# Two convolution projection chunks of a Conformer/MoBA block as one seven-product block

## The chip, the cores and the metric

The kernel is one launch on one core of one Trainium2 chip. The metric is the device time of that launch in microseconds, the median of several runs. Everything is float32 in and out. A matrix product is made of three TensorE products of float32r parts (high x high, low x high, high x low).

## The reference

A decoder block on x (256 tokens of 2048 columns): a SwiGLU feed-forward network, a token mixer, a second feed-forward network, each with a residual and a layer norm. The mixer's input projection has 12288 columns; its `u` part feeds the convolution.

```python
z = h @ w_in
q, k, v, u, ga, gc = jnp.split(z, list(np.cumsum(IN_SPLITS)[:-1]), axis=-1)
o = moba_attention(to_heads(q), to_heads(k), to_heads(v))
y_attn = o.transpose(0, 2, 1, 3).reshape(B, S, ATTN_WIDTH) @ w_attn_out
# conformer_conv
a, g = jnp.split(u, 2, axis=-1)
h = a * jax.nn.sigmoid(g)
h = conv_general_dilated(h, w_dw, 31 causal taps per channel, 1024 channels) + b_dw
h = jax.nn.silu(layer_norm(h, ln_g, ln_b))
y_conv = h @ w_pw2
return (jax.nn.sigmoid(ga) * y_attn + jax.nn.sigmoid(gc) * y_conv) @ w_out
```

## The kernel before

**Groups.** Weights come in groups of 4 row blocks of 128 by 512 columns (1 MB). For group n, SyncE loads it into one of eight slots `g_raw`, ScalarE writes its high part (`g_split`, L817) and VectorE the low part (`g_lo_of`, L1338) into place n % 4 of a ring (`RING` = 4), and TensorE multiplies it with the token factors `xF_hi`/`xF_lo` (L2259 to L2261). ScalarE may write group n only when TensorE has finished group n-4 (`g_used`), and a slot is loaded again when the low part of its last user is made. All four engines and the queues walk orders written out by hand, and semaphores tie them.

**Direct and seven-product.** A chunk is 512 columns of the projection. Direct, it takes four groups, each against both token tiles: 24 matmuls a group. In a "full" block two chunks (g and u) share a Strassen-Winograd scheme of seven products with 14 groups of 12 matmuls, P1a to P4b, where a and b are the two halves of a product's depth. The scheme needs sums of weight groups. VectorE makes some in place (`add`, L1346, semaphore `t_ready`), GpSimd makes others by a DMA that reads a group from memory and adds it onto a slot (`add_from_hbm`, L2102). It also needs copies of PSUM banks (`fork`, L899) and subtractions (`values`, L1819).

**The mixer's order.** After the first network's norm come the convolution's four chunks, all direct: gate columns, value columns, for the first and the second 512 channels (`CONV_CHUNKS`). ScalarE takes the sigmoid (`conv_gate`, L1084), VectorE the product (`conv_value`, L1760), TensorE turns it (`turn_conv`, L2245) and ScalarE puts it into `ch` (`conv_block`, L1077). Then six blocks of the mixer (`mixing_block`), each the 14 groups of two chunks and 4 direct groups Q1 to Q4 of a third. Blocks 0 to 3 project the keys, values and queries of four heads each; blocks 4 and 5 project gate columns. The attention of the four heads of block g-1 runs inside block g (blocks 1 to 4, the head blocks): keys and queries are transposed by VectorE (L1824), written to memory and read back by GpSimd's queue (L2140, L2147), copied by ScalarE (`qT`, L1108) and multiplied by TensorE (`scores`, L2544). Then eight direct groups of gate columns (the gate groups), then `attn_out`, `conv_out` and `mix_out`, whose weights go in units through `raw`, `w_hi`, `w_lo` (L767, L1315), and whose four `attn_out` chunks share one pair of banks that VectorE empties (`attn_rows`, L1950).

**Taps.** The 31 taps of each of 8 channel tiles are 248 VectorE instructions on 128x256 (L1774, L1777), two tiles in turn with one accumulator each (`cacc`). They are spread by hand over the VectorE order: 33 around the last convolution groups, 16 in block 0, 16 in each head block, 17 in the last block, 8 or 6 behind each gate group, 3 behind each unit of `attn_out`, the last 2 at one place in its third chunk:

```python
lo_conv(13)
dve.wait_ge(cw_loaded, 32)
dve.wait_ge(kept_out, 16 * TT * ND)
taps(11)
lo_conv(14)
taps(11)
lo_conv(15)
taps(11)
```

`BLOCK_TAPS` gives ten places a block: behind Q1, P5a, P3b, P7b, Q3, P4a, P2a, P2b, P4b and behind `values`.

## Time and profile before

| | us |
|---|---|
| median of 3 runs | 2113.19 (2112.93 to 2113.49) |
| span of the profiled execution | 2109.5 |
| TensorE busy | 2095.7 (99%) |
| TensorE weight loads busy | 1734.6 (82%) |
| VectorE busy | 1877.2 (89%) |
| ScalarE busy | 1402.9 (67%) |
| GpSimd busy | 216.7 (10%) |
| DMA engines, mean | 264 GB/s |

The span runs from the first to the last instruction of one profiled execution; the median of the timed runs lies 3.7 us above it, and no other time is known of that execution. Matmuls overlap in the record, so TensorE's pace is read from the distance between their starts. In a timeline the number in brackets is the engine's idle time before a row, with what ended it.

### The profile page before, as it was taken

To read this page: it belongs to the slowest core of one execution; us is meant where nothing else is said; L and a number is where in the kernel's file an instruction comes from. 1 tells how busy PE (TensorE), PEld (TensorE's weight loads), DVE (VectorE), ACT (ScalarE), POOL (GpSimd) and SP (SyncE) were. 2 spreads that over 40 slices of the span, in tenths; PEclk is the share of its full clock that TensorE was granted. 3 is DMA by queue.
4 is the path that set the end of the run, shared out by engine and by line. 5 is a ranking of instruction groups with operands and counts; after the bars stand their busy time and mean duration, and the time that the engine had idled before them with its cause. 6 is when DMAs were issued, how large, how long until landed. Compare 5 with 4: busy or idle time off the path is not lost.

```text
span 2109.5 us, 23778 instructions
## 1 busy us (share of the span) xinstructions
PE 2095.7 (99%) x9386; PEld 1734.6 (82%) x9386; DVE 1877.2 (89%) x1420; ACT 1402.9 (67%) x1313; POOL 216.7 (10%) x345
## 2 busy tenths in 40 slices
PE   9999999999999999999999999999999999999998
PEld 7888888888888888888888888888888888888886
DVE  7899999999996889999999986659899999999996
ACT  6677777777775546766676445335677777777773
POOL 0111111101110001011100000000111111100110
PEclk9999999999999999999999999999999999999999
DMA  9798988888985759998898556755788988899892
GB/s 369 253 295 260 279 270 266 291 300 277 289 279 231 276 158 311 299 269 270 304 301 262 212 185 240 260 178 200 244 294 255 282 272 267 290 302 278 288 285 113
DMA packets 92397, 556.65 MB, mean 264 GB/s; under 512 B 13056, under 2 KB 13440, under 8 KB 35200
## 3 DMA queue, kind: packets, MB, share of 16 engines
q1 hardware_dynamic: 68544, 437.69, 54.7%
q0 software_dynamic: 23744, 117.46, 25.8%
q8 instruction: 74, 1.21, 0.2%
q14 instruction: 35, 0.29, 0.0%
HBM read 534.13 MB, written 20.97 MB: 263 GB/s over the span
## 4 chain that ended last, share of the span: by engine, by line
PE 88%; DVE 8%; DMA 2%; ACT 1%; issue 1%; SPq 0%; DVEq 0%; ACTq 0%
PE acc L2259 14%; PE acc L2261 14%; PE acc L2260 14%; PE tb L2259 12%; PE tb L2261 12%; PE tb L2260 12%; PE acc L2197 3%; PE acc L2199 3%; PE acc L2198 3%; DVE g_lo L1338 3%; DVE cacc L1777 3%; DMA g_raw<-in_groups 1%; PE tb L2245 1%; DVE w_lo L1315 1%; DVE g_raw L1346 1%
## 5 line engine op out<-in xcount | busy, mean ns | idle before, releaser
L1338 DVE TENSOR_TENSOR g_lo<-g_raw,g_hi 128x2048 fp32r<-128x2048 f32 x506 | 1147.6, 2286 | 120.4 <-ACT g_hi L817 119.8
L817 ACT ACTIVATE g_hi<-g_raw 128x2048 fp32r<-128x2048 f32 x506 | 964.4, 1916 | 319.8 <-DVE g_raw L1346 121.5
L2259 PE MATMUL acc<-g_hi,xF_hi 128*128 128x512 f32 x1184 | 464.3, 392 | 0.6 <-ACT acc L899 0.6
L2261 PE MATMUL acc<-g_hi,xF_lo 128*128 128x512 f32 x1184 | 461.1, 389 | 0.0
L2260 PE MATMUL acc<-g_lo,xF_hi 128*128 128x512 f32 x1184 | 460.7, 389 | 0.0
L2259 PE MATMUL tb<-g_hi,xF_hi 128*128 128x512 f32 x760 | 296.3, 390 | 0.3 <-DVE g_lo L1338 0.2
L2261 PE MATMUL tb<-g_hi,xF_lo 128*128 128x512 f32 x760 | 295.7, 389 | 0.0
L2260 PE MATMUL tb<-g_lo,xF_hi 128*128 128x512 f32 x760 | 295.7, 389 | 0.0
L1346 DVE TENSOR_TENSOR g_raw<-g_raw,g_raw 128x2048 f32<-128x2048 f32 x120 | 274.3, 2286 | 1.3
L2259 PEld LDWEIGHTS acc<-g_hi,xF_hi 128*128 128x128 f32 x1184 | 222.3, 188 | 46.8 <-ACT acc L899 1.0
L2261 PEld LDWEIGHTS acc<-g_hi,xF_lo 128*128 128x128 f32 x1184 | 222.2, 188 | 46.8
L2260 PEld LDWEIGHTS acc<-g_lo,xF_hi 128*128 128x128 f32 x1184 | 222.4, 188 | 45.1
L2259 PEld LDWEIGHTS tb<-g_hi,xF_hi 128*128 128x128 f32 x760 | 142.7, 188 | 30.4 <-issue 1.1
L2261 PEld LDWEIGHTS tb<-g_hi,xF_lo 128*128 128x128 f32 x760 | 142.6, 188 | 29.8
L2102 POOL DMA_DIRECT2D g_raw<-in_groups x80 | 72.5, 941 | 918.8 <-DVE g_lo L1338 870.6
L2260 PEld LDWEIGHTS tb<-g_lo,xF_hi 128*128 128x128 f32 x760 | 142.7, 188 | 29.4
L767 ACT ACTIVATE w_hi<-raw 128x1024 fp32r<-128x1024 f32 x80 | 84.7, 1062 | 105.0 <-DMA raw<-in_stream 65.4
L2259 PE MATMUL tb<-g_hi,hT_hi 128*128 128x512 f32 x384 | 149.8, 390 | 0.0
L2261 PE MATMUL tb<-g_hi,hT_lo 128*128 128x512 f32 x384 | 149.4, 389 | 0.0
L2260 PE MATMUL tb<-g_lo,hT_hi 128*128 128x512 f32 x384 | 149.4, 389 | 0.0
L2259 PE MATMUL acc<-g_hi,hT_hi 128*128 128x512 f32 x320 | 124.7, 390 | 0.0
L2261 PE MATMUL acc<-g_hi,hT_lo 128*128 128x512 f32 x320 | 124.5, 389 | 0.0
(180 smaller groups left out, 2307.7 us busy)
## 6 DMA issues: line engine op xcount, KB each, us to landing
g_raw<-in_groups SPq DMA_DIRECT2D x356, 1024.0 KB, 7.2
g_raw<-in_groups POOLq DMA_DIRECT2D x80, 1024.0 KB, 8.6
raw<-in_stream SPq DMA_DIRECT2D x80, 512.0 KB, 4.5
bounce<-h_sq POOLq DMA_DIRECT2D x40, 256.0 KB, 5.5
h_in<-bounce POOLq DMA_DIRECT2D x160, 64.0 KB, 2.6
ln_gb<-in_ln SPq DMA_DIRECT2D x6, 1024.0 KB, 6.6
g_raw<-in_groups SPq DMA_DIRECT2D x6, 512.0 KB, 9.7
res<-in_x_rows SPq DMA_DIRECT2D x1, 2048.0 KB, 16.6
```

Source lines behind the costliest of these rows:

```text
L767: act.activation(w_hi[:, seg.split(j)], raw[:, seg.raw(j)], ACT.Copy).then_inc(hi_ready, 1)
L817: act.activation(g_hi[:, n % RING], source[:], ACT.Copy).then_inc(g_hi_ready, 1)
L1338: dve.tensor_tensor(g_lo[:, n % RING], source[:], f32(g_hi[:, n % RING]), ALU.subtract).then_inc(g_lo_ready, 1)
L1346: dve.tensor_tensor(out[:], a[:], b[:], ALU.add).then_inc(t_ready, 1)
L1777: ins = dve.scalar_tensor_tensor(out=rows if j == TAPS - 1 else cacc[:, k], in0=rows, scalar=w, in1=cacc[:, k], op0=ALU.mult, op1=ALU.add)
L2102: pool.dma_start(out=source(f, b, onto)[:].rearrange("p k n -> p (k n)"), in_=groups[k], accum_op=ALU.add).then_inc(ready, 16)
L2197: pe.matmul(out_ap, x[0][:, k, rows], w_hi[:, s, cols], start=begin, stop=False)
L2198: pe.matmul(out_ap, x[0][:, k, rows], w_lo[:, s, cols], start=False, stop=False)
L2199: return pe.matmul(out_ap, x[1][:, k, rows], w_hi[:, s, cols], start=False, stop=end)
L2259: pe.matmul(bank, x_hi_ap, g_hi[:, n % RING, blk], start=begin, stop=False, skip_group_check=True)
L2260: pe.matmul(bank, x_hi_ap, g_lo[:, n % RING, blk], start=False, stop=False, skip_group_check=True)
L2261: return pe.matmul(bank, x_lo_ap, g_hi[:, n % RING, blk], start=False, stop=end, skip_group_check=True)
```

## The change

The convolution's third and fourth chunk (gate and value columns of the second 512 channels) are no longer two direct chunks of four groups but one seven-product block of 14 groups, `conv_pair`, numbered block -1. Two of its sums are T1a and T1b (`add` of ra onto qa, rb onto qb), two more T2a and T2b, all on VectorE, and four are adding DMAs. Its value part comes out of `values` into `vt`, its gate part out of two sigmoids (`conv_gate_out`) into `k_sb`, and their product is made in block 0 behind Q1 (`conv_pair_value`). TensorE turns it there behind Q1 too, where it stood ahead of Q1. The 33 taps that stood around the last convolution groups go: 3 to block 0, 3 to each of the four head blocks, 3 to the last block, 8 to the gate groups, and 7 are left over for the place of the last ones in `attn_out`, which has 9 now. `TAP_ROUNDS` still takes the tiles two by two with two accumulators. `SPLIT0` and the counts of some semaphores follow the new number of groups.

```diff
-SPLIT0 = 2
+SPLIT0 = 6
...
+PAIR = ("P1a", "P1b", "P5a", "P5b", "P6a", "P3a", "P6b", "P3b", "P7a", "P7b", "P2a", "P4a", "P4b", "P2b")
+PAIR_LOADS = {"qa": "P4a", "ra": "P7a", "qb": "P4b", "rb": "P7b", "ua": "P3a", "ub": "P3b", "ga": "P2a", "gb": "P2b"}
...
 MIXING_SUMS = ("T1a", "T3a", "T2a", "T2b")
+PAIR_SUMS = ("T1a", "T1b", "T2a", "T2b")
+CONV = -1
 Q_COL, K_COL, V_COL, U_COL, GA_COL, GC_COL = 0, D, 2 * D, 3 * D, 3 * D + 2 * CC, 4 * D + 2 * CC
-CONV_CHUNKS = (U_COL + CC, U_COL, U_COL + CC + COLS, U_COL + COLS)
+CONV_CHUNKS = (U_COL + CC, U_COL)
+PAIR_CHUNKS = (U_COL + CC + COLS, U_COL + COLS)
...
-HEAD_TAPS = (0, 0, 0, 0, 2, 2, 3, 3, 3, 3)
-BLOCK_TAPS = ((3, 3, 1, 1, 3, 1, 1, 1, 1, 1), *([HEAD_TAPS] * NG), (1, 1, 2, 2, 1, 2, 2, 2, 2, 2))
+HEAD_TAPS = (0, 0, 0, 0, 3, 3, 3, 3, 3, 4)
+BLOCK_TAPS = ((3, 3, 2, 2, 3, 1, 1, 2, 1, 1), *([HEAD_TAPS] * NG), (1, 1, 3, 3, 2, 2, 2, 2, 2, 2))
+TAP_ROUNDS = ((0, 1), (2, 3), (4, 5), (6, 7))
...
+        self.number("mix", CONV, True)
+        for m, name in enumerate(PAIR):
+            self.at["mix", CONV, name] = n + m
+        for name, last in PAIR_LOADS.items():
+            self.load_at["mix", CONV, name] = len(self.order)
+            matrix, p = WEIGHTS[name]
+            self.load("mix", PAIR_CHUNKS["gu".index(matrix)], p, self.at["mix", CONV, last])
+        for name in PAIR_SUMS:
+            sums += 1
+            self.sum_no["mix", CONV, name] = sums
+        n += len(PAIR)
...
+            def conv_pair():
+
+                f, g = "mix", CONV
+                split_loaded(f, g, "P1a", "qa")
+                split_loaded(f, g, "P1b", "qb")
+                split_sum(f, g, "P5a", "qa", "T1a")
+                split_sum(f, g, "P5b", "qb", "T1b")
+                fork(f, g, acc[:, BY], acc[:, BX], "P1b")
+                split_sum(f, g, "P6a", "qa", "T2a")
+                split_loaded(f, g, "P3a", "ua")
+                split_sum(f, g, "P6b", "qb", "T2b")
+                act.wait_ge(acc_out[1], 2)
+                fork(f, g, acc[:, BZ], acc[:, BW], "P5b")
+                split_loaded(f, g, "P3b", "ub")
+                conv_block(0)
+                act.wait_ge(t3a_ready, 16)
+                split(f, g, "P7a", "ra")
+                act.wait_ge(t3b_ready, fulls(f, g))
+                split(f, g, "P7b", "rb")
+                save_value(g, 0, "P6b")
+                split_loaded(f, g, "P2a", "ga")
+                act.wait_ge(t4a_ready, fulls(f, g))
+                split(f, g, "P4a", "qa")
+                act.wait_ge(t4b_ready, 16)
+                split(f, g, "P4b", "qb")
+                save_value(g, 1, "P7b")
+                split_loaded(f, g, "P2b", "gb")
+
+            def conv_gate_out(t):
+
+                act.wait_ge(g_used, mix_used(CONV, ("P2b", "P4b")[t]))
+                act.activation(k_sb[:, t], acc[:, (BY, BX)[t]], ACT.Sigmoid).then_inc(k_out, 1)
+
             def mixing_block(g):
 
                 f = "mix"
                 heads = 0 < g <= NG
+                if not g:
+                    conv_gate_out(1)
                 split_loaded(f, g, "P1a", "qa")
                 if g:
                     keys_out(g - 1, 0)
+                else:
+                    conv_gate_out(0)
                 split_loaded(f, g, "P1b", "qb")
                 if g:
                     keys_out(g - 1, 1)
...
             factors_hi("mix")
             split_conv(7)
             conv_gate(0)
-            for g in range(8, 15):
-                split_conv(g)
-            conv_block(0)
-            split_conv(15)
-            conv_gate(1)
+            conv_pair()
             act.wait_ge(kept_out, 16 * TT * ND)
...
+            def tap(m):
+
+                for n, tiles in enumerate(TAP_ROUNDS):
+                    if m < TAPS * len(tiles):
+                        j, k = m // len(tiles), m % len(tiles)
+                        return j, k, tiles[k], len(tiles if j or not n else TAP_ROUNDS[n - 1])
+                    m -= TAPS * len(tiles)
+
             def taps(count):
 
                 for m in range(taps_done[0], min(taps_done[0] + count, KC * TAPS)):
-                    pair, n = m // (2 * TAPS), m % (2 * TAPS)
-                    k, j = n % 2, n // 2
-                    c = 2 * pair + k
-                    if n == 0:
-                        dve.wait_ge(ch_ready, 2 if pair < 2 else 4)
+                    j, k, c, behind = tap(m)
+                    if j == 0 and k == 0:
+                        dve.wait_ge(ch_ready, 2 if c == 0 else 4)
                     rows = ch[:, c, j:j + T]
                     w = cw[:, c * TAPS + j:c * TAPS + j + 1]
-                    dve.wait_ge(conv_step, m + 1)
+                    dve.wait_ge(conv_step, max(2, m + 3 - behind))
                     if j == 0:
-                        ins = dve.tensor_scalar(cacc[:, k], rows, w, cw[:, KC * TAPS + c:KC * TAPS + c + 1],
+                        ins = dve.tensor_scalar(taps_sum[k], rows, w, cw[:, KC * TAPS + c:KC * TAPS + c + 1],
                                                 ALU.mult, ALU.add)
                     else:
-                        ins = dve.scalar_tensor_tensor(out=rows if j == TAPS - 1 else cacc[:, k], in0=rows,
-                                                       scalar=w, in1=cacc[:, k], op0=ALU.mult, op1=ALU.add)
+                        ins = dve.scalar_tensor_tensor(out=rows if j == TAPS - 1 else taps_sum[k], in0=rows,
+                                                       scalar=w, in1=taps_sum[k], op0=ALU.mult, op1=ALU.add)
                     ins.then_inc(conv_step, 1)
                 taps_done[0] += count
...
+            def conv_pair():
+
+                f, g = "mix", CONV
+                qa, qb, ra, rb, ua, ub = (source(f, g, name) for name in ("qa", "qb", "ra", "rb", "ua", "ub"))
+                lo_group(f, g, "P1a", "qa")
+                load_done(f, g, "ra")
+                split_done(f, g, "P1a")
+                add(qa, qa, ra)
+                lo_group(f, g, "P1b", "qb")
+                load_done(f, g, "rb")
+                split_done(f, g, "P1b")
+                add(qb, qb, rb)
+                lo_group(f, g, "P5a", "qa")
+                load_done(f, g, "ua")
+                split_done(f, g, "P5a")
+                add(qa, qa, ua)
+                conv_value(0)
+                lo_group(f, g, "P5b", "qb")
+                load_done(f, g, "ub")
+                split_done(f, g, "P5b")
+                add(qb, qb, ub)
+                lo_group(f, g, "P6a", "qa")
+                lo_group(f, g, "P3a", "ua")
+                lo_group(f, g, "P6b", "qb")
+                lo_group(f, g, "P3b", "ub")
+                lo_group(f, g, "P7a", "ra")
+                lo_group(f, g, "P7b", "rb")
+                lo_group(f, g, "P2a", "ga")
+                lo_group(f, g, "P4a", "qa")
+                lo_group(f, g, "P4b", "qb")
+                lo_group(f, g, "P2b", "gb")
+                values(g)
+
+            def conv_pair_value():
+
+                dve.wait_ge(k_out, TT)
+                dve.wait_ge(v_out, TT)
+                for t in range(TT):
+                    dve.tensor_tensor(act_sb[:, t], k_sb[:, t], vt[:, t], ALU.mult).then_inc(acc_out[1], 1)
 
...
                 if not g:
-                    conv_value(1)
+                    conv_pair_value()
...
-            lo_conv(8)
-            lo_conv(9)
-            lo_conv(10)
-            conv_value(0)
-            lo_conv(11)
-            lo_conv(12)
-            lo_conv(13)
+            conv_pair()
             dve.wait_ge(cw_loaded, 32)
             dve.wait_ge(kept_out, 16 * TT * ND)
-            taps(11)
-            lo_conv(14)
-            taps(11)
-            lo_conv(15)
-            taps(11)
             dve.wait_ge(alibi_loaded, 16)
             for g in range(BLOCKS):
                 mixing_block(g)
 
             for g in range(PIECES * GATES):
                 lo_gate(g)
-                taps(6 if g - 1 in HEADS_AT else 8)
+                taps(7 if g - 1 in HEADS_AT else 9)
...
+            def conv_pair_sums():
+
+                f, g = "mix", CONV
+                pool.wait_ge(t_ready, G.sum_no[f, g, "T1a"])
+                add_from_hbm(f, g, "ra", "ua", t3a_ready)
+                pool.wait_ge(t_ready, G.sum_no[f, g, "T1b"])
+                add_from_hbm(f, g, "rb", "ub", t3b_ready)
+                pool.wait_ge(g_lo_ready, lo_count(G.at[f, g, "P6a"]))
+                add_from_hbm(f, g, "qa", "ga", t4a_ready)
+                pool.wait_ge(g_lo_ready, lo_count(G.at[f, g, "P6b"]))
+                add_from_hbm(f, g, "qb", "gb", t4b_ready)
...
+            def conv_pair():
+
+                f, g = "mix", CONV
+                X, Y, Z, W = (acc[:, bank] for bank in (BX, BY, BZ, BW))
+                pe.wait_ge(acc_out[0], 2)
+                product_group(f, g, "P1a", X, A11, 0, begin=True)
+                product_group(f, g, "P1b", X, A11, 1)
+                pe.wait_ge(x_lo, 11 + 4 * factors("mix"))
+                pe.wait_ge(acc_out[1], 2)
+                product_group(f, g, "P5a", W, S1, 0, begin=True)
+                product_group(f, g, "P5b", W, S1, 1)
+                turn_conv(0)
+                wait_fork(f, g, 0)
+                product_group(f, g, "P6a", X, S2, 0)
+                wait_fork(f, g, 1)
+                product_group(f, g, "P3a", Z, S4, 0)
+                product_group(f, g, "P6b", X, S2, 1)
+                product_group(f, g, "P3b", Z, S4, 1)
+                wait_fork(f, g, 2)
+                product_group(f, g, "P7a", X, S3, 0)
+                product_group(f, g, "P7b", X, S3, 1)
+                product_group(f, g, "P2a", Y, A12, 0)
+                wait_fork(f, g, 3)
+                product_group(f, g, "P4a", X, A22, 0)
+                product_group(f, g, "P4b", X, A22, 1)
+                product_group(f, g, "P2b", Y, A12, 1)
+
             def mixing_block(g):
 
                 f = "mix"
                 heads = 0 < g <= NG
                 X, Y, Z, W = (acc[:, bank] for bank in (BX, BY, BZ, BW))
-                if g:
-                    pe.wait_ge(k_out, 2 * g)
-                else:
-                    pe.wait_ge(acc_out[0], 4)
+                pe.wait_ge(k_out, evicted(g - 1) if g else 1)
                 product_group(f, g, "P1a", X, A11, 0, begin=True)
                 product_group(f, g, "P1b", X, A11, 1)
                 if g:
                     pe.wait_ge(q_out, 2 * g)
-                else:
+                query_group(g, 0)
+                if not g:
                     turn_conv(1)
-                query_group(g, 0)
...
             plain_chunk(conv + PIECES, (acc[:, 2], acc[:, 3]))
-            pe.wait_ge(acc_out[0], 2)
-            pe.wait_ge(x_lo, 11 + 4 * factors("mix"))
-            plain_chunk(conv + 2 * PIECES, (acc[:, 0], acc[:, 1]), after={(3, 0): lambda: turn_conv(0)})
-            pe.wait_ge(acc_out[1], 2)
-            plain_chunk(conv + 3 * PIECES, (acc[:, 2], acc[:, 3]))
+            conv_pair()
```

**ScalarE where the pair ends and block 0 begins.** `g_hi` is a group's high part, `act_sb<-acc` the second gate chunk's sigmoid (before) or a saved bank (now), `k_sb<-acc` the new sigmoids. Before:

```order
L1077 ACTIVATE ch<-tb 128x4x128 x2
L817 ACTIVATE g_hi<-g_raw_64 128x2048
L1084 ACTIVATE act_sb<-acc 128x512 x2
L817 ACTIVATE g_hi<-g_raw_60 128x2048
L817 ACTIVATE g_hi<-g_raw_62 128x2048
L817 ACTIVATE g_hi<-g_raw_66 128x2048
L817 ACTIVATE g_hi<-g_raw_61 128x2048
```

Now, from P4b on:

```order
L839 ACTIVATE g_hi<-g_raw_62 128x2048
L921 ACTIVATE act_sb<-acc 128x512
L839 ACTIVATE g_hi<-g_raw_66 128x2048
L1189 ACTIVATE k_sb<-acc 128x512
L839 ACTIVATE g_hi<-g_raw_67 128x2048
L1189 ACTIVATE k_sb<-acc 128x512
L839 ACTIVATE g_hi<-g_raw_60 128x2048
L839 ACTIVATE g_hi<-g_raw_61 128x2048
```

The first `k_sb` waits for P4b on TensorE and stands ahead of block 0's P1a (slot 67); the second waits for P2b and stands ahead of P1b. Before, the two sigmoids stood ahead of P1a (slot 60) as well, but they waited for the third chunk, four groups back on TensorE.

**VectorE from the first group of the pair.** Before:

```order
L1338 TENSOR_TENSOR g_lo<-g_raw_64,g_hi 128x2048
L1338 TENSOR_TENSOR g_lo<-g_raw_60,g_hi 128x2048
L1338 TENSOR_TENSOR g_lo<-g_raw_62,g_hi 128x2048
L1760 TENSOR_TENSOR act_sb<-act_sb,acc 128x512 x2
L1338 TENSOR_TENSOR g_lo<-g_raw_63,g_hi 128x2048
```

Now:

```order
L1390 TENSOR_TENSOR g_lo<-g_raw_64,g_hi 128x2048
L1398 TENSOR_TENSOR g_raw_64<-g_raw_64,g_raw_60 128x2048
L1390 TENSOR_TENSOR g_lo<-g_raw_62,g_hi 128x2048
L1398 TENSOR_TENSOR g_raw_62<-g_raw_62,g_raw_63 128x2048
L1390 TENSOR_TENSOR g_lo<-g_raw_64,g_hi 128x2048
L1398 TENSOR_TENSOR g_raw_64<-g_raw_64,g_raw_66 128x2048
L1812 TENSOR_TENSOR act_sb<-act_sb,acc 128x512 x2
L1390 TENSOR_TENSOR g_lo<-g_raw_62,g_hi 128x2048
L1398 TENSOR_TENSOR g_raw_62<-g_raw_62,g_raw_67 128x2048
```

Between the low parts of P1a, P1b, P5a and P5b now stand four additions, and the product of the first half stands behind the third of them.

## Rows read from the trace of the kernel before

**Rows 1.** The page, part 1: busy us (share) and instructions.
```profile
PE 2095.7 (99%) x9386; PEld 1734.6 (82%) x9386; DVE 1877.2 (89%) x1420; ACT 1402.9 (67%) x1313; POOL 216.7 (10%) x345
```
**Rows 2.** Timeline of PE: start us, us, instruction; 48 matmuls from first to last.
```profile
659.49 0.39 PE L2259 MATMUL acc<-g_hi,hT_hi 128*128 128x512 f32 x1
...
670.37 0.39 PE L2259 MATMUL acc<-g_hi,hT_hi 128*128 128x512 f32 x1
```
**Rows 3.** Waits of PE: us in total, times, longest us.
```profile
PE tb L2544 <- issue: 0.8, 1, 0.8
PE acc L2197 <- DVE sig_a L1950: 0.7, 1, 0.7
PE acc L2259 <- ACT acc L899: 0.6, 1, 0.6
```
**Rows 4.** Timeline of DVE around the conv chunks.
```profile
714.55 4.49 DVE L1338 TENSOR_TENSOR g_lo<-g_raw,g_hi 128x2048 fp32r<-128x2048 f32 x2
...
746.38 0.73 DVE L1774 TENSOR_SCALAR cacc<-ch,cw 128x256 f32<-128x256 f32 x2 [7.00 <-ACT ch L1077]
```
**Rows 5.** Timeline of DVE in block 0: low part, additions.
```profile
779.31 2.29 DVE L1338 TENSOR_TENSOR g_lo<-g_raw,g_hi 128x2048 fp32r<-128x2048 f32 x1
781.64 2.29 DVE L1346 TENSOR_TENSOR g_raw<-g_raw,g_raw 128x2048 f32<-128x2048 f32 x1
...
789.44 2.28 DVE L1346 TENSOR_TENSOR g_raw<-g_raw,g_raw 128x2048 f32<-128x2048 f32 x1
```
**Rows 6.** Timeline of ACT: high parts released by PE, and a sigmoid or copy between.
```profile
723.36 1.92 ACT L817 ACTIVATE g_hi<-g_raw 128x2048 fp32r<-128x2048 f32 x1 [0.80 <-PE acc L2261]
...
768.06 1.92 ACT L817 ACTIVATE g_hi<-g_raw 128x2048 fp32r<-128x2048 f32 x1 [0.80 <-PE acc L2261]
...
821.75 0.60 ACT L1089 ACTIVATE k_sb<-acc 128x512 f32<-128x512 f32 x1 [0.74 <-PE acc L2261]
822.24 1.91 ACT L817 ACTIVATE g_hi<-g_raw 128x2048 fp32r<-128x2048 f32 x1
```
**Rows 7.** The chain of waits: start us, us, what.
```profile
728.71 0.87 PE tb L2245 x8
...
794.22 0.50 PE acc L2259
...
1246.56 0.50 PE acc L2197
```
**Rows 8.** Timeline of DVE in the gate groups and the first unit behind.
```profile
1158.43 3.27 DVE L1777 SCALAR_TENSOR_TENSOR cacc<-ch,cw,cacc 128x256 f32<-128x256 f32 x8
1161.60 2.30 DVE L1338 TENSOR_TENSOR g_lo<-g_raw,g_hi 128x2048 fp32r<-128x2048 f32 x1
...
1196.45 1.23 DVE L1315 TENSOR_TENSOR w_lo<-raw,w_hi 128x1024 fp32r<-128x1024 f32 x1 [1.16 <-ACT w_hi L767]
```
**Rows 9.** Timelines of ACT, PE and DVE: queries and scores of blocks 2, 3, 4.
```profile
915.16 1.15 ACT L1108 ACTIVATE qT<-q_sq 128x512 f32<-128x512 f32 x2 [4.04 <-DMA q_sq<-q_bounce]
916.41 0.46 PE L2544 MATMUL tb<-kT,qT 128*128 128x128 f32 x2 [0.79 <-issue]
...
966.82 1.30 DVE L1824 STREAM_TRANSPOSE q_sq<-act_sb 128x512 f32<-128x512 f32 x2
...
981.93 1.16 ACT L1108 ACTIVATE qT<-q_sq 128x512 f32<-128x512 f32 x2 [2.95 <-DMA q_sq<-q_bounce]
983.53 0.38 PE L2544 MATMUL tb<-kT,qT 128*128 128x128 f32 x2
...
1047.83 1.15 ACT L1108 ACTIVATE qT<-q_sq 128x512 f32<-128x512 f32 x2 [1.79 <-DMA q_sq<-q_bounce]
...
1050.25 0.38 PE L2544 MATMUL tb<-kT,qT 128*128 128x128 f32 x2
```
**Rows 10.** DMA issues from 700 to 900 us: count, KB, median us to landing.
```profile
g_raw<-in_groups POOLq DMA_DIRECT2D x8, 1024.0 KB, 13.1
```
**Rows 11.** The page, part 6: the same over the whole program.
```profile
g_raw<-in_groups POOLq DMA_DIRECT2D x80, 1024.0 KB, 8.6
```

More of the change, by code:

```diff
@@ L392, in build @@
         cacc = mix("cacc", [P, 2, T])
+        taps_sum = [cacc[:, 0], cacc[:, 1]]
         assert at[0] <= x_at
@@ L495, in build @@
         stored = sem("stored")
-        u_gates = 2
-        u1_attn = u_gates + GATES // 2
-        u0_convo = u_gates + GATES - GATES // 2
+        u0_gates, u1_gates = 1, 2
+        u1_attn = u1_gates + GATES // 2
+        u0_convo = u0_gates + GATES - GATES // 2
         u0_mix = u0_convo + ND
@@ L557, in gate_use, with evicted @@
         def gate_use(c):
-            return u_gates + c // 2
+            return (u0_gates, u1_gates)[gate_pair(c)] + c // 2
+        def evicted(g):
+            return TT * (g - CONV + 1)
         def gate_rows_of(c):
@@ L1094, in queries_out @@
                 if g < NG:
-                    act.wait_ge(v_out, 2 * g + 2)
+                    act.wait_ge(v_out, evicted(g))
                 for t in range(TT):
@@ L1173, in mixing_block @@
                 if g:
-                    act.wait_ge(t3a_ready, 16 * g)
+                    act.wait_ge(t3a_ready, 16 * (g + 1))
                     split(f, g, "P7a", "ra")
@@ L1246, in _ @@
             split_gate(3)
-            act.wait_ge(v_out, 2 * BLOCKS)
+            act.wait_ge(v_out, evicted(BLOCKS - 1))
             for t in range(TT):
@@ L2180, in _ @@
             keep_rows()
+            conv_pair_sums()
             for g in range(BLOCKS):
@@ L2638, in _ @@
                 if c < 2:
-                    pe.wait_ge((v_out, k_out)[c], 2 * BLOCKS)
+                    pe.wait_ge((v_out, k_out)[c], evicted(BLOCKS - 1))
                 else:
@@ L2646, in turn_conv_out @@
             def turn_conv_out(half):
-                pe.wait_ge(conv_step, BLK * TAPS * (half + 1) + 2)
+                pe.wait_ge(conv_step, TAPS * (next(r for r in TAP_ROUNDS if BLK * half + BLK - 1 in r)[-1] + 1) + 2)
                 pe.wait_ge(q_out, 2 * BLOCKS)
```

18 lines of the change are left out of this document (6 added, 12 removed).

## Prediction

> **What bounds the kernel now.** I read the busy shares, then TensorE's own waits, then the timelines of the engines around each wait. TensorE is busy 99% of the span [rows 1], but a busy matmul row says little by itself, since matmuls overlap. The distance between starts says it: from 659.49 to 670.37 lie 48 matmuls of 512 columns, so one costs 0.227 us [rows 2], a group of 12 costs 2.72 us and a group of 24 costs 5.44 us. In the stages of the change TensorE loses only three stalls: 0.6 us at the copy of a bank in block 0, 0.8 us before the scores of a head block and 0.7 us at the gate product of attn_out [rows 3]. So each matmul taken away is worth its 0.227 us, as long as the other engines feed TensorE sooner too. VectorE decides that. It makes each group's low half in 2.20 us (two in 4.49 us less 0.09 us of overlap [rows 4]), so against a product group of 2.72 us it has 0.5 us to spare, and each addition (2.20 to 2.33 us, from 779.31 to 781.64 [rows 5]) eats four such spares. Around the conv chunks it still has air: before the first tap it stands idle 7.00 us [rows 4].
>
> **The change, part by part.** A "shift" below is TensorE's place against the traced execution.
>
> *The pair.* Two direct chunks take 8 x 24 matmuls, the block 14 x 12: 24 fewer, 5.4 us. Traced, TensorE passes from the end of the first two chunks to the first group of block 0 in 768.06 - 723.36 = 44.7 us [rows 6]; the block needs 14 x 2.72 + 0.87 for eight transposes [rows 7] = 39.0 us. That is **-5.7 us** without waits. VectorE's work there grows by 6 low halves, 4 additions and 2 subtractions of 512 columns, and 33 taps leave. It starts P1a at 714.55 as before [rows 4], since nothing ahead of it changes. It then runs split, addition three times and the conv value: 3 x (2.33 + 2.20) + 1.3 = 14.9 us, so to 729.4. TensorE wants P5a at 723.3 + 5.4 = 728.7 but waits there for that conv value: +0.7. Next come split P5b, addition and split P6a: 729.3 + 2.33 + 2.20 + 2.29 = 736.1, against 729.5 + 5.44 + 0.87 = 735.8 on TensorE: +0.4 with the release. From P6a on VectorE has no addition and gains 0.5 us a group. The pair's waits are **+1.2 us**; P4b ends at 760.8, P2b at 763.5.
>
> *The hand-over to block 0.* ScalarE's new order puts the sigmoid of P4b's bank ahead of block 0's first g_hi. Elsewhere Q4, 5.44 us on TensorE, lies between; the pair has no Q4. The path is half a sigmoid pair 0.5 (821.75 to 822.24), g_hi 1.92 [rows 6], g_lo 2.29 [rows 4], releases some 0.2: 760.8 + 4.9 = 765.7 against 763.5, **+2.2 us**. Then the other sigmoid waits for P2b, so g_hi of P1b runs 764.1 to 766.0, g_lo to 768.3, the addition to 770.5, g_lo of Q1 to 772.7. TensorE is there at 765.7 + 5.4 = 771.1: **+1.6 us**. In the trace that addition starts at 768.12, now at 768.2, with the same work behind it: VectorE is back at its old clock. The next point where TensorE needs it is the copy before P3a, released by the addition at 789.44 [rows 5] through ScalarE's copy to the matmul at 794.22 [rows 7]. All that stands 0.1 us later, so TensorE waits another 1.6 us there and at P5b. It lost 0.8 us there before (the row's 0.6, which counts from a matmul's 0.39 us end, and the 0.16 us by which matmuls overlap): **+0.8 us**. Sum so far -5.7 + 1.2 + 2.2 + 1.6 + 0.8 = **+0.1 us**: the gain is gone by P3a of block 0.
>
> *Taps.* One costs 0.396 us (eight between 1158.43 and 1161.60 [rows 8]); still two accumulators, so the pace stays. Block 0 gets 3 more, all before VectorE's idle ahead of P4b: 0. The last block gets 3, before waits on ScalarE too: 0. The four head blocks get 3 each, before P4a, before P2a and behind the values; the idle that would take them comes later, ahead of P3a. So VectorE reaches the transposition of keys and queries 1.2 us later in blocks 2, 3 and 4. From there the queries go through memory and back: transposition at 966.82, qT at 981.93 to 983.09, scores on TensorE at 983.53 [rows 9], a spare of some 0.35 us, so +0.85. In block 2 TensorE already waits (qT until 916.31, scores at 916.41 [rows 9]): +1.2. In block 4 qT ends at 1048.98 and the scores start at 1050.25 [rows 9]: 1.2 us to spare, 0. Block 1 has as much. **+2.0 us**, bounded by 0 (the round trip takes it up) and 3 x 1.2 = 3.6 (none does). Keys go ahead of the queries on the same queue and shift with them.
>
> *Gate groups.* VectorE runs from 1146.7 to the gate product at 1245.8 almost without idle, and TensorE waits for that product (1246.56 [rows 7]). Each of 8 groups gets one tap; the eighth falls into the 1.16 us that VectorE waits for w_hi at 1196.45 [rows 8]. The next load follows the seventh's low half, so it moves along: 7 x 0.396 = **+2.8 us**, part of it as a stall in attn_out's first units. Seven further taps (2.8 us) come behind the product, with about 7 us until the conv rows are turned: 0. Bounds are 2.0 and 3.2.
>
> *Adding DMAs.* GpSimd issues four more 1 MB loads that add onto a slot, in a stretch with room. The last, for P4b, is issued at about 741. In this stretch such a load took 13.1 us in the median [rows 10], over the whole program 8.6 us [rows 11]. By these it lands at 749.6 or at 754.1; split and low half (4.2 us) put it at 758.4 in the worse case, against 758.1 on TensorE: 0 to 0.3 us. I take 0, since only two are in flight. The Trainium skill, "DMA: Bandwidth & Descriptors", section "Anatomy of one DMA — SWDGE (gpsimd) path", fits such a DMA by 2.0 us plus bytes over 436e3, an estimate of 4.4 us for 1 MB; by it this term could not exist at all, and the trace does not agree with it here.
>
> **Sum:** +0.1 + 2.0 + 2.8 = +4.9 us. The span goes from 2109.5 [rows 1] to 2114.4 us; the median lies 3.7 us above the span, so 2113.2 + 4.9 = **2118.1 us**. A measurement of this kernel tells about 0.2%, 4.2 us, from no change: the forecast is just past it, at +0.23%.
>
> **Rivals.**
> (B) *Part of the delay is covered.* The queries' way through memory took 15 to 17 us, so it varies by more than the 1.2 us that I add, and the two-digit spares may hide it. Without the term of the head blocks the time is 2116.1 us. Against: in block 2 TensorE waits already.
> (C) *The hand-over keeps some gain.* If VectorE does not fall back to its old clock in block 0, half of the waits there (2.8 us) vanish: 2115.3 us. Against: the addition chain is fixed by the order.
> (D) *Faster.* TensorE's work alone decides: the 33 taps that leave let VectorE stay ahead through block 0, so its old 0.8 us goes as well. Place: g_lo of P1a in block 0. The price is -5.7 - 0.8 = -6.5 us, 2106.7 us. It decides if that g_lo ends by 763.5 instead of 765.7 and the gate groups lose nothing. For: 7.00 us of idle before the taps [rows 4]. Against: the sigmoid ahead of the first g_hi.
> (E) *The adding DMAs queue.* From 8.6 to 13.1 us is one step of queueing; one step more makes 17.6 us, and P4b is ready at 741 + 17.6 + 4.2 = 762.8 instead of 758.1. That is 4.7 us, and block 0 follows P4b: 2122.8 us. For: the plain loads of block 0 all start in the same 20 us. Against: only two such DMAs are in flight.
> (F) *The matmuls do not go.* The built order has 24 rows fewer on TensorE (8950 for 8974), so this is settled.
>
> **How the numbers follow.** Forecast 0.50 (its own range 2116.0 to 2120.5), B 0.17, C 0.10, D 0.08, E 0.15. Slower by over 0.2% means above 2117.4: seven tenths of the forecast's half (0.35) and E, 0.50. Faster by over 0.2% is D, 0.08. The rest, 0.42, lies within. The range leaves D and E's far end out: 2112.5 to 2121.5 us.
>
> **What would show it.** Right: a stall of about 2 us at block 0's first matmul behind ScalarE's k_sb and VectorE's g_lo, another of 1.6 us at Q1, the matmul behind the bank copy within 0.5 us of 794.2; waits before the scores of about 2.0 us in block 2 and 0.9 us in block 3; VectorE idle nowhere in the gate groups and the stalls of attn_out at 3 to 3.5 us in all. Wrong: P1a of block 0 without a stall (then C or D), the scores unchanged (B), or TensorE waiting for a g_hi behind an adding DMA (E).

## The result and the profile after

The changed kernel takes 2122.6 us (2122.0 to 2124.7, four runs) against 2113.1 us for the kernel before on the same chip: 1.0048 times as long, 95% interval 1.0034 to 1.0063, so **9.5 us slower**. The forecast was 2118.1 us, and its range ended at 2121.5 us.

The page after, parts of it that answer to [rows 1]:

```profile
PE 2093.7 (99%) x9362; PEld 1731.0 (82%) x9362; DVE 1900.8 (90%) x1432; ACT 1415.1 (67%) x1323; POOL 220.4 (10%) x349
```

TensorE's waits in the stages of the change, 700 to 1300 us (us in total, times, longest); they answer to [rows 3]:

```profile
PE tb L2644 <- issue: 4.6, 4, 2.5
PE acc L2359 <- DVE g_lo L1390: 2.6, 2, 2.3
PE acc L2297 <- DVE w_lo L1367: 1.8, 3, 0.7
PE acc L2297 <- DVE sig_a L2037: 1.4, 1, 1.4
PE tb L2359 <- DVE g_lo L1390: 1.2, 1, 1.2
PE acc L2359 <- ACT acc L921: 1.1, 1, 1.1
PE acc L2359 <- ACT act_sb L921: 1.1, 1, 1.1
PE acc L2359 <- issue: 1.0, 1, 1.0
PE tb L2345 <- ACT pT L1146: 0.4, 1, 0.4
```

Before, the same list came to 2.3 us. Now it comes to 15.2 us. It says who is waited for; the cost of a stage comes better from TensorE's own starts. Cut at three places (the first matmul of the pair, or of the third conv chunk; the end of Q4 of block 0; the end of Q4 of block 4), and with the last block at 59.8 us in every trace, the traces give the table below. The kernels from the third row on are those of the experiments.

| us | pair and block 0 | head blocks 1 to 4 | behind the last block | span |
|---|---|---|---|---|
| before | 106.6 | 268.2 | 951.5 | 2109.5 |
| changed | 108.5 | 274.5 | 955.1 | 2120.5 |
| pair_only | 109.0 | 272.6 | 950.9 | 2115.7 |
| taps_only | 105.2 | 271.4 | 954.6 | 2113.7 |
| gate_behind | 105.4 | 273.3 | 957.4 | 2118.5 |
| save_ahead | 107.3 | 276.4 | 955.4 | 2121.9 |
| heads_idle | 107.9 | 270.7 | 955.2 | 2116.9 |
| gate_taps_back | 108.0 | 274.1 | 952.0 | 2116.8 |
| before_idle | 106.6 | 267.6 | 952.0 | 2109.8 |
| combined | 103.2 | 271.6 | 950.5 | 2108.2 |
| load_held | 107.9 | 281.8 | 954.3 | 2127.1 |
| before_held | 106.6 | 279.5 | 952.2 | 2121.1 |
| combined2 | 103.2 | 269.6 | 950.6 | 2106.4 |
| combined_held | 103.4 | 275.4 | 950.5 | 2111.8 |

So the change costs 1.9 us in the pair and block 0, 6.3 us in the head blocks and 3.6 us behind, less 0.7 us by which that trace was ahead of the other when the pair began. Those are 11.0 us of span and 9.5 us of median. In the profiled executions of all kernels run since, the time lies 1.7 to 1.9 us above the span. By that the trace of before, at 2109.5 us, was an execution of 2111.3 us, 1.8 us better than its median. Where it gained them can't be read from one trace, but its write of the queries' squares in block 4, 6.3 us from issue to landing, is the shortest of all traces but the three in which a load is held back. Two other traces lie far from their medians: that of `pair_only` is 2.0 us above and that of `save_ahead` 3.4 us above; the rest lie within 0.9 us. The kernel before alone took 2109.7 to 2115.8 us in 65 later executions on three chips, so a difference between two lines of the table counts only where the rows of the traces show its cause.

**The pair.** TensorE's rows with a wait in brackets, at P4a of the pair, and then P1a, Q1 and P3a of block 0 (one timeline, start, duration):

```profile
756.28 0.50 PE L2359 MATMUL acc<-g_hi,xF_hi 128*128 128x512 f32 x1 [1.06 <-ACT act_sb L921]
...
767.13 0.47 PE L2359 MATMUL acc<-g_hi,xF_hi 128*128 128x512 f32 x1 [2.35 <-DVE g_lo L1390]
...
773.99 0.50 PE L2359 MATMUL tb<-g_hi,xF_hi 128*128 128x512 f32 x1 [1.18 <-DVE g_lo L1390]
...
795.40 0.50 PE L2359 MATMUL acc<-g_hi,xF_hi 128*128 128x512 f32 x1 [1.09 <-ACT acc L921]
```

The last three are the waits of the forecast. The first is not in it. ScalarE and GpSimd around it:

```profile
753.83 1.92 ACT L839 ACTIVATE g_hi<-g_raw 128x2048 fp32r<-128x2048 f32 x1 [4.75 <-DMA g_raw<-in_groups]
755.65 0.57 ACT L921 ACTIVATE act_sb<-acc 128x512 f32<-128x512 f32 x1
```

```profile
740.61 0.86 POOL L2189 DMA_DIRECT2D g_raw<-in_groups  x1 [3.64 <-DVE g_lo L1390]
```

P4b's adding DMA is issued at 740.61 and lets ScalarE go on at 753.83, 13.2 us later, about the 13.1 us of [rows 10]. P4b itself does not suffer. But ScalarE waits for that load ahead of its copy of P7b's bank (755.65), and TensorE needs the copy before P4a may write the bank. P4a starts at 756.28, 1.45 us behind the matmul before it, where 0.23 us is the usual distance; with the slower start of the next one that is 1.3 us lost.

**The head blocks.** In block 2 GpSimd writes the queries' squares to memory at 903.99 and may fetch them back at 914.31:

```profile
901.70 2.22 POOL L2234 DMA_DIRECT2D kT<-k_bounce  x4 [2.74 <-DMA k_bounce<-kT]
903.99 0.56 POOL L2227 DMA_DIRECT2D q_bounce<-q_sq  x1
914.31 2.18 POOL L2234 DMA_DIRECT2D q_sq<-q_bounce  x4 [9.76 <-DMA q_bounce<-q_sq]
```

In the trace of before the same write took 2 us less:

```profile
902.19 0.56 POOL L2140 DMA_DIRECT2D q_bounce<-q_sq  x1
910.66 2.19 POOL L2147 DMA_DIRECT2D q_sq<-q_bounce  x4 [7.92 <-DMA q_bounce<-q_sq]
```

From issue to landing the write takes 9.5, 10.0, 8.4 and 8.3 us in blocks 1 to 4, where it took 7.5, 8.2, 8.1 and 6.3 us. It leaves 1.5 us later against TensorE in block 3 alone, and within 0.3 us of its old place in the others. In blocks 2 and 4 the keys do leave 1.1 to 1.3 us later, as forecast, but their own way through memory was shorter by as much or more.

In block 2 TensorE then waits 2.50 us for the scores (start of the first one, and of the matmuls around it):

```profile
917.17 0.39 PE L2361 MATMUL acc<-g_hi,xF_lo 128*128 128x512 f32 x1
920.06 0.60 PE L2644 MATMUL tb<-kT,qT 128*128 128x128 f32 x2 [2.50 <-issue]
920.45 0.64 PE L2645 MATMUL tb<-kT,qT 128*128 128x128 f32 x2
...
923.02 0.63 PE L2360 MATMUL acc<-g_lo,xF_hi 128*128 128x512 f32 x1
...
924.00 0.39 PE L2360 MATMUL acc<-g_lo,xF_hi 128*128 128x512 f32 x1
```

Behind the wait matmuls start some 0.43 us apart, and only from 924 us on 0.23 us again. The windows (duration; busy time and count of PE, PEld, DVE, ACT, POOL; then the granted clock, the DMA share and GB/s) tell why:

```profile
917.00:920.00 3.00, 0.56 (x3) 0.13 (x1) 2.04 (x1) 1.19 (x3) 2.26 (x3) 1.00 0.81 161
920.00:924.00 4.00, 3.94 (x16) 3.71 (x17) 2.21 (x1) 3.56 (x2) 0.00 (x0) 0.57 1.02 207
924.00:928.00 4.00, 4.00 (x19) 3.33 (x18) 3.33 (x4) 1.92 (x2) 0.31 (x1) 1.00 1.02 219
```

Behind the wait the granted clock is 0.57 in the mean of 4 us, that is 0.5 (1.2 GHz) for 3.4 us of them. By these figures it costs 4 x (1 - 0.57) = **1.7 us** more. The trace of before has no such drop between 700 and 1300 us.

### The profile page after: what moved, and what is told of

It reads as the page before. It is cut to its first block, busy times and chain, and to the rows that moved or that the text cites. A ratio compares the mean times of both kernels' runs of the same rounds, so it can differ in the third digit from the quotient of the medians.

```text
span 2120.5 us, 23774 instructions
## 1 busy us (share of the span) xinstructions
PE 2093.7 (99%) x9362; PEld 1731.0 (82%) x9362; DVE 1900.8 (90%) x1432; ACT 1415.1 (67%) x1323; POOL 220.4 (10%) x349
## 4 chain that ended last, share of the span: by engine, by line
PE 88%; DVE 8%; DMA 2%; issue 1%; ACT 1%; SPq 0%; DVEq 0%; ACTq 0%
PE acc L2359 14%; PE acc L2361 14%; PE acc L2360 14%; PE tb L2359 12%; PE tb L2361 12%; PE tb L2360 12%; DVE g_lo L1390 3%; PE acc L2297 3%; PE acc L2298 3%; PE acc L2299 3%; DVE cacc L1835 2%; DMA g_raw<-in_groups 2%; DVE w_lo L1367 1%; PE tb L2345 1%; PE acc L2413 1%
## 5 line engine op out<-in xcount | busy, mean ns | idle before, releaser
L1390 DVE TENSOR_TENSOR g_lo<-g_raw,g_hi 128x2048 fp32r<-128x2048 f32 x512 | 1160.5, 2284 | 120.6 <-ACT g_hi L839 120.3
L839 ACT ACTIVATE g_hi<-g_raw 128x2048 fp32r<-128x2048 f32 x512 | 975.3, 1915 | 299.7 <-DVE g_raw L1398 125.1
L1398 DVE TENSOR_TENSOR g_raw<-g_raw,g_raw 128x2048 f32<-128x2048 f32 x124 | 283.3, 2285 | 1.7
```

The costliest lines, as they stand in the source:

```text
L839: act.activation(g_hi[:, n % RING], source[:], ACT.Copy).then_inc(g_hi_ready, 1)
L1390: dve.tensor_tensor(g_lo[:, n % RING], source[:], f32(g_hi[:, n % RING]), ALU.subtract).then_inc(g_lo_ready, 1)
L1398: dve.tensor_tensor(out[:], a[:], b[:], ALU.add).then_inc(t_ready, 1)
```

## The experiments

**Each part alone.** `pair_only`, in short:

```diff
-HEAD_TAPS = (0, 0, 0, 0, 3, 3, 3, 3, 3, 4)
+HEAD_TAPS = (0, 0, 0, 0, 2, 2, 3, 3, 3, 3)
+LEFT_OUT = 33
-                for m in range(taps_done[0], min(taps_done[0] + count, KC * TAPS)):
+                for m in range(taps_done[0], min(taps_done[0] + count, KC * TAPS - LEFT_OUT)):
-                taps(7 if g - 1 in HEADS_AT else 9)
+                taps(6 if g - 1 in HEADS_AT else 8)
```

> The changed kernel with the pair, but the tap counts of every block and gate group as in the kernel before; the last 33 of the 248 taps are left out, so the last two conv tiles are not finished. Theory (the taps in the head blocks cost 6.3 us and those in the gate groups 3 us, the pair and its hand-over about 2 us): 2115 us, scores of blocks 1 to 4 waited for as before (TensorE's group P5b 4.1, 5.1, 4.1, 4.1 us), attn_out's stalls 0.7 us. Rival (the pair itself puts the queries' trip through memory at another place against the loads, and the taps only add their 0.4 us each): 2118 us or more, with P5b of block 2 at 6.5 us or more.

`taps_only` is the kernel before with these edits (and the changed kernel's counts in `BLOCK_TAPS` and the gate groups):

```diff
-            taps(11)
             lo_conv(14)
-            taps(11)
             lo_conv(15)
-            taps(11)
```

> The kernel before with direct conv chunks, but the 33 taps moved out of them to where the change puts them. Theory (taps cost 6.3 + 3 us): 2121 to 2122 us, P5b of block 2 near 8 us on TensorE. Rival as in the run with the pair alone (the taps cost what the prediction gave them, 2.0 + 2.8): 2118 us, with waits before the scores 1.2 us longer in block 2 and 0.85 us in block 3.

Measured: 2115.5 us for the pair (1.0014, 1.0005 to 1.0023) and 2115.8 us for the taps (1.0018, 1.0009 to 1.0027), against 2112.2 us. By the medians the two parts cost 3.3 and 3.6 us, 6.9 us together, where the changed kernel loses 9.5; the intervals are too wide to call the rest a cost of having both. The theory was within 0.5 us for the pair's time but not for its waits, and for the taps both theory and rival were too high. In the trace the taps cost 3.2 us in the head blocks, not 6.3, and 3.1 us behind. In block 0 that trace is 1.4 us shorter: TensorE's losses there fall from 1.5 to 0.3 us, with the 33 taps no longer ahead of it. And the pair costs something in the head blocks with no tap added there, 4.4 us in this trace (which is 2.0 us above its median). Its waits for the scores:

```profile
PE tb L2645 <- issue: 4.0, 3, 1.6
```

Four traces now say how long the write of the queries' squares takes in block 1, where it and the loads beside it differ by at most 0.4 us in their place against TensorE: 7.5 us (before), 8.3 (taps_only), 9.5 (changed), 10.1 (pair_only). I took that for spread of the transfer, but the later traces speak for a part that comes with the pair. In block 1 the write took 7.5 to 8.5 us in the three traces without the pair and without the hold described below, and 9.5 to 10.1 us in seven of the eight with it (7.9 in `gate_behind`). In block 2 it took 7.7 to 8.2 us in the three and 9.9 to 11.0 us in all eight. There the order of the transfers differs as well: without the pair the write of the keys' squares took 3.9 to 4.9 us and their reads were issued behind the plain load, with the pair it took 2.9 us and the first two reads went ahead of the load. So the rival, that the pair puts the queries' trip at another place against the loads, fits block 2, though no run tests it alone. In block 1 nothing in the issues explains the difference.

In the same trace of the pair the clock fell at the first wait of block 0 too:

```profile
764.00:768.00 4.00, 2.02 (x9) 1.32 (x8) 2.07 (x1) 3.74 (x3) 0.00 (x0) 1.00 1.01 424
768.00:772.00 4.00, 3.63 (x9) 2.94 (x10) 3.74 (x3) 4.00 (x3) 0.75 (x2) 0.57 0.29 117
```

That is the same wait of 2.35 us that the changed kernel has in its own trace without a drop.

**ScalarE's two orders.** `gate_behind`:

```diff
-                if not g:
-                    conv_gate_out(1)
                 split_loaded(f, g, "P1a", "qa")
                 if g:
                     keys_out(g - 1, 0)
                 else:
-                    conv_gate_out(0)
+                    conv_gate_out(1)
                 split_loaded(f, g, "P1b", "qb")
                 if g:
                     keys_out(g - 1, 1)
+                else:
+                    conv_gate_out(0)
```

> The changed kernel with ScalarE's sigmoid of P4b's bank behind the high half of block 0's P1a instead of ahead of it, and that of P2b's bank behind P1b's. Theory (the sigmoid ahead of the first high half is the hand-over's cost, and VectorE's chain carries it on): no stall at P1a, 1.3 us left at Q1, P3a 2.5 us earlier, 2120.1 us. Rival (VectorE's additions are late anyway, so the stall only moves from P1a to Q1 and the bank copy before P3a): P3a as before, 2122.5 us.

`save_ahead`:

```diff
+                save_value(g, 1, "P7b")
                 act.wait_ge(t4b_ready, 16)
                 split(f, g, "P4b", "qb")
-                save_value(g, 1, "P7b")
```

> The changed kernel with ScalarE's copy of P7b's bank to SBUF ahead of its wait for P4b's adding DMA. Theory (TensorE's P4a waits 1.4 us for that copy, which stands behind the DMA in ScalarE's order): P4a without a stall, everything after it 1.3 us earlier, 2121.3 us. Rival (P4b's own operand comes from that DMA, so the stall moves to P4b): P4b's end as now, 2122.6 us.

Measured: 2120.9 us (1.0041, 1.0028 to 1.0055) and 2120.3 us (1.0038, 1.0024 to 1.0051). The intervals overlap that of the changed kernel, so only the traces can tell. With `gate_behind` the low half of P1a starts at 761.10, directly behind the value parts, and pair and block 0 take 3.0 us less (105.4 for 108.5), where the theory said 2.5. The rival falls:

```profile
759.90 1.28 DVE L1877 TENSOR_TENSOR vt<-acc,act_sb 128x512 f32<-128x512 f32 x2
761.10 2.28 DVE L1390 TENSOR_TENSOR g_lo<-g_raw,g_hi 128x2048 fp32r<-128x2048 f32 x1
764.11 2.29 DVE L1390 TENSOR_TENSOR g_lo<-g_raw,g_hi 128x2048 fp32r<-128x2048 f32 x1 [0.73 <-ACT g_hi L839]
```

With `save_ahead` no wait for `act_sb` is left at P4a, and the stage is 1.2 us shorter, as said, although the clock fell in it. Not all of it reaches the end. `gate_behind` gives 2.3 us back at attn_out, where the product's wait is longer and the clock falls behind it:

```profile
PE acc L2297 <- DVE sig_a L2037: 2.3, 1, 2.3
```

```profile
1250.00:1255.00 5.00, 2.74 (x12) 1.98 (x11) 5.00 (x10) 2.12 (x2) 0.00 (x0) 1.00 0.70 233
1255.00:1259.00 4.00, 4.00 (x12) 3.10 (x12) 4.00 (x10) 1.06 (x1) 0.00 (x0) 0.57 0.47 155
```

**The taps at another place.** `heads_idle`:

```diff
-HEAD_TAPS = (0, 0, 0, 0, 3, 3, 3, 3, 3, 4)
+HEAD_TAPS = (0, 0, 0, 0, 2, 2, 3, 3, 3, 3, 3)
                 add(qb, qb, ub)
+                if heads:
+                    taps(counts[10])
                 lo_group(f, g, "P3a", "ua")
```

> The changed kernel with the 12 taps that the change adds to the head blocks moved ahead of the low half of P3a, where VectorE stands idle 2.4 to 2.7 us, three in each block. Theory (they put the queries 1.3 us later against TensorE, and the queries' trip has no spare left in the mean, so each head block from the second on pays 1.3 us): the queries' transposition is back at its old distance to TensorE, the groups P5b of blocks 2 to 4 take some 4.9 us in the mean instead of 6.2, 2118.6 us. Rival (the trip's own spread, 6.3 to 11 us for the write, makes these waits, the taps hardly): P5b as in the changed kernel, 2122 us.

`gate_taps_back` changes only `taps(7 if ... else 9)` back to `taps(6 if ... else 8)` in the gate groups.

> The changed kernel with 6 and 8 taps behind the gate groups' low halves as before; the 8 more come behind the gate product. Theory (VectorE runs without idle from the gate groups to the product, so each tap there is 0.4 us late for TensorE): the first units of attn_out wait for w_lo no more, the product's stall is 0.7 us, 2119.4 us. Rival (the taps behind the product delay the conv rows or attn_out's last units): 2121 us or more, with new waits behind 1260 us.

Measured: 2118.7 us (1.0036, 1.0022 to 1.0049) and 2118.4 us (1.0031, 1.0019 to 1.0042), against 2112.3 us. That is 6.5 and 6.1 us slower than before instead of 9.5; the intervals still overlap that of the changed kernel. The times and the traces fit both theories. In `heads_idle` three taps fit into the idle with 1.44 us to spare, and the head blocks take 3.8 us less:

```profile
916.09 2.28 DVE L1398 TENSOR_TENSOR g_raw<-g_raw,g_raw 128x2048 f32<-128x2048 f32 x1
918.29 1.27 DVE L1835 SCALAR_TENSOR_TENSOR cacc<-ch,cw,cacc 128x256 f32<-128x256 f32 x3
920.99 2.29 DVE L1390 TENSOR_TENSOR g_lo<-g_raw,g_hi 128x2048 fp32r<-128x2048 f32 x1 [1.44 <-ACT g_hi L839]
```

In `gate_taps_back` the three waits for w_lo are gone and one is left between 1150 and 1300 us; 3.1 us are saved, and the eight more taps behind the product cost nothing that can be read:

```profile
PE acc L2297 <- DVE sig_a L2037: 1.0, 1, 1.0
```

**The kernel before, with taps in its idle.** `before_idle` has the same place ahead of P3a, with `HEAD_TAPS = (0, 0, 0, 0, 2, 1, 1, 2, 2, 2, 6)`.

> The kernel before with 6 of the 16 taps of each head block moved ahead of the low half of P3a. Theory (the queries leave 2.4 us earlier and the scores are never waited for): P5b 4.1 us in all four head blocks, the span 1 us shorter, runs closer together, 2111.2 us. Rival (the write of the squares then meets the plain loads and takes longer, or P3a's low half comes late): 2112.2 us or more.

Measured: 2111.4 us against 2112.3 (0.9997, 0.9988 to 1.0006), which can't be told from no change. One wait of 0.5 us before scores is left where the trace of before had 0.8. The queries left at most 0.3 us earlier against TensorE, not 2.4, since ahead of P1a and of P1b VectorE then waits for ScalarE's high halves:

```profile
888.56 2.29 DVE L1338 TENSOR_TENSOR g_lo<-g_raw,g_hi 128x2048 fp32r<-128x2048 f32 x1 [0.43 <-ACT g_hi L817]
891.34 2.29 DVE L1338 TENSOR_TENSOR g_lo<-g_raw,g_hi 128x2048 fp32r<-128x2048 f32 x1 [0.48 <-ACT g_hi L817]
```

**What the collision is.** `load_held`, for the head blocks:

```diff
+            behind_queries = {G.load_at["mix", g, "ub"]: g for g in range(1, NG + 1)}
             def load_mixing(first, last):
+                    if k in behind_queries:
+                        sp.wait_ge(q_sent, 16 * behind_queries[k])
                     load_group(k)
```

> The changed kernel, but in each head block SyncE issues the plain load of ub only when the queries' squares are in memory (it was issued 1.5 us before that write). Theory (the write of the squares, 256 KB, takes 8.3 to 11.0 us because it shares the DMA engines with that 1 MB load; the squares of the keys, with no load beside them, take 2.9 us): the write takes 6 us or less, P5b takes 4.1 us in all four head blocks, 2116.6 us. Rival (it queues behind the four loads of the keys issued just ahead of it on the same queue): write as long as before, P5b as in the changed kernel, 2122 us or more where ub then comes late.

`before_held` is the kernel before with these lines.

> The kernel before with the same hold of ub's load. Theory: the write takes 6 us or less instead of 6.3 to 8.2, the wait of 1.0 us before the scores of block 2 goes, 2111.2 us. Rival as there: 2112.2 us, or more if ub comes late.

Measured: 2128.9 us (1.0078, 1.0064 to 1.0092) and 2122.6 us (1.0042, 1.0028 to 1.0055): more than 10 us above the expectations of 2116.6 and 2111.2 us. And yet the theory was right about what makes the write long. GpSimd in block 2 of `load_held`:

```profile
905.31 0.56 POOL L2231 DMA_DIRECT2D q_bounce<-q_sq  x1
910.37 2.18 POOL L2238 DMA_DIRECT2D q_sq<-q_bounce  x4 [4.50 <-DMA q_bounce<-q_sq]
912.54 1.88 POOL L2193 DMA_DIRECT2D g_raw<-in_groups  x2
```

The write is over in 5.1 us instead of 10.3 (3.7 to 4.8 us from issue to landing in the four blocks, 8.3 to 10.0 without the hold), so the plain loads beside it are what made it long. The write is of 512 KB; the 256 KB of the expectation is wrong. But the load of ub, and the next one right behind it, now start together with the four reads back. The last of these lands 9.5 us after its issue, where it took 2.8 to 3.0 us. Against TensorE the queries are back 1.2 to 2.2 us later than without the hold. TensorE's waits before the scores are 10.9 us in all, and behind two of them the clock fell. The rival named the right side for a reason that was not its own: it had the write as long as before.

**All together.** `combined`, in short, has both of ScalarE's orders, `taps(10)` in the pair behind P4a's low half, no tap ahead of P3a in block 0, six ahead of P3a in each head block, and 6 or 7 in the gate groups:

```diff
                 lo_group(f, g, "P4a", "qa")
+                taps(10)
                 lo_group(f, g, "P4b", "qb")
-HEAD_TAPS = (0, 0, 0, 0, 3, 3, 3, 3, 3, 4)
-BLOCK_TAPS = ((3, 3, 2, 2, 3, 1, 1, 2, 1, 1), *([HEAD_TAPS] * NG), (1, 1, 3, 3, 2, 2, 2, 2, 2, 2))
+HEAD_TAPS = (0, 0, 0, 0, 1, 2, 2, 2, 2, 3, 6, 1)
+BLOCK_TAPS = ((0, 0, 3, 3, 4, 2, 2, 3, 1, 1, 0, 0), *([HEAD_TAPS] * NG), (1, 2, 2, 2, 1, 2, 2, 2, 2, 2, 1, 4))
-                taps(7 if g - 1 in HEADS_AT else 9)
+                taps(6 if g - 1 in HEADS_AT else 7)
```

> The changed kernel with both of ScalarE's orders of the runs before (sigmoid behind P1a's high half, P7b's copy ahead of the DMA wait), ten taps in the pair behind P4a's low half while VectorE waits for P4b's load, six ahead of P3a in each head block, none before P3a in block 0, and 52 behind the gates' low halves. Theory (each cost found is on its own and they add): 3.0 + 1.2 us from the hand-over, about 1 from block 0's bank copy, 6 from the head blocks, 3 from the gates: 2108 us. Rival (the stalls hide each other, and the 24 matmuls come back as waits for VectorE): 2112 us, as the kernel before.

`combined2` takes five taps out of block 0, `(0, 0, 3, 3, 3, 1, 1, 1, 1, 1, 0, 0)`. They come behind the gate product, where the kernel before has two, `combined` eight and this one thirteen; the six and twelve of its expectation are miscounted.

> The combined kernel with six fewer taps behind P3a of block 0 and six more behind the gate product (twelve there in all). Theory (in the combined kernel the six taps moved within block 0 sent the queries of block 1 1.6 us later, which cost 2.7 us at its scores): P5b of block 1 at 4.1 to 5.3 us, 2108.4 us. Rival (twelve taps behind the product are late for the turning of the conv rows): new waits behind 1260 us, 2110.9 us.

`combined_held` adds the hold of `load_held`.

> The same as combined2, and ub's load held as in the other two. Theory: no wait before any scores, 2107 us, and its runs closer together. Rival: as combined2.

Measured: `combined` 2110.9 us (0.9997, 0.9988 to 1.0006), `combined2` **2108.8 us (0.9981, 0.9972 to 0.9990)**, `combined_held` 2113.6 us (1.0005, 0.9996 to 1.0014). `combined` is between its two theories: pair and block 0 take 103.2 us, 3.4 less than before, so the pair pays at last. Part of that is due to the taps, not the pair: `taps_only`, with direct chunks, has 105.2 us there. And `combined` has a wait of its own in block 1, where the taps put later in block 0 had made the queries 1.6 us late:

```profile
PE tb L2647 <- issue: 3.4, 2, 2.5
```

`combined2` takes that away and lands 0.4 us from its expectation. It is the one version whose whole interval lies below the kernel before, by 3.4 us in the medians (2112.2 us beside it) and by 0.19% in the ratio. All its waits between 720 and 1300 us:

```profile
PE tb L2647 <- issue: 1.5, 2, 0.9
PE acc L2362 <- issue: 1.0, 1, 1.0
PE tb L2362 <- DVE g_lo L1390: 0.9, 1, 0.9
PE tb L2348 <- ACT pT L1146: 0.4, 1, 0.4
PE acc L2362 <- DVE g_lo L1390: 0.3, 1, 0.3
```

The hold costs 4.8 us there as well.

## Why the prediction was wrong

The direction and the three places were right, but the sum of +4.9 us was about half of what came. Two steps failed. The first is that the head blocks were charged for the taps alone, at +2.0 us: there the pair itself, put at nothing, and the half clock behind a wait, put at nothing too, made it 6.3 us. The second is that only P4b was asked whether its adding DMA comes in time: ScalarE's wait for that DMA cost 1.3 us at P4a.

- **The pair**: the waits at P5a and P6a came, 1.3 and 0.4 us from start to start for 0.7 and 0.4 forecast. But the step "the pair's waits are +1.2 us" lacked the 1.3 us at P4a. I had the load right ([rows 10], "758.4 in the worse case") and asked only whether P4b's operand would be in time. What stood behind the waiting instruction on ScalarE, the copy of P7b's bank, was not asked. It is rival E's cause at another place and at less than a third of E's price. `save_ahead` shows it.
- **Hand-over to block 0**: the mechanism was right. P1a costs 2.6 us from start to start (2.2 forecast), Q1 1.5 (1.6), P3a half a microsecond more than before (0.8 at P5b and P3a together). "VectorE is back at its old clock" was wrong by 1.3 us: the addition starts at 769.5, not 768.2, since the first high half hangs on P4b's end. So pair and block 0 came to +1.9 us, not +0.1. `gate_behind` shows that the sigmoid's place alone is worth 3.0 us. Rivals C and D fall with the traced waits; C was priced wrongly too, since half of the forecast's 4.6 us of waits is 2.3 us, not 2.8.
- **Head blocks**: the step "+2.0 us, bounded by 0 and 3.6" failed. The taps alone cost 3.2 us in `taps_only`, and 3.8 us by `heads_idle` against the changed kernel, of which 1.7 us is the clock. That is near or above the bound for "none is taken up". The pair alone, which had no term here, lengthened the head blocks by 4.4 us in `pair_only`; in `heads_idle`, with its taps out of the queries' way, they are still 2.5 us longer than before. The forecast had waits of 2.0 us in block 2 and 0.9 in block 3. They were 2.5 and 0.9, and blocks 1 and 4 waited 0.5 and 0.6 us, where a full 1.2 us to spare had been read. The spare of block 4 came from one execution with a write of 6.3 us; in the changed kernel it took 8.3. And a wait was priced at its length, although the one of 2.5 us in block 2 had 1.7 us of half clock behind it. Rival B, that the delay is covered, falls: I had named the spread and drawn the wrong end from it.
- **Gate groups**: the mechanism was right, +2.8 us forecast against 3.6 us behind the last block, of which `gate_taps_back` returns 3.1. The stalls of attn_out are 3.2 us in all, within the 3 to 3.5 forecast. The nine taps at the last place of attn_out cost nothing that can be read, nor do the seventeen of `gate_taps_back`.
- **Adding DMAs**: the 13.1 us were right (13.2 us). The price that the Trainium skill gives in "DMA: Bandwidth & Descriptors", section "Anatomy of one DMA — SWDGE (gpsimd) path", 4.4 us as estimated in the forecast, is a third of it; the trace does not agree with it where plain loads run beside.
- **Trace and median**: 3.7 us between the median and the span was taken for a fixed part. Some 1.8 us of that are fixed and some 1.8 us are a lucky execution, so some of what I called the kernel's spare may have been its luck.

What stays open: why the write of the squares takes 7.5 to 8.5 us in block 1 without the pair and mostly 9.5 to 10.1 with it, at the same place; how much of the pair's 2.5 to 4.4 us in the head blocks is that and how much is chance, since each kernel has one trace; and how often the clock falls in the runs without a profile.

## What to carry to other kernels

A stall moved past an in-order engine is not only late for its own consumer: list everything behind the waiting instruction, and ask of each who waits for it. A spare that is read from one trace of a transfer with spread may be gone in the next execution, and a change upstream can move the transfers that it was read beside. Where several transfers share the engines, holding one back can move the collision to the next. Extra work belongs into idle that lies behind the last send of a round trip, not ahead of it: the same twelve taps cost 3.8 us more ahead of the queries than in the idle behind them, by the traces, and 3.1 us more by the medians against the kernel before.
